# Two chained blocks on one core: steps reordered at two branch ends, in the wide feed-forward network and in attention

## The chip, the cores and the metric

The kernel runs on 1 core of one Trainium2 chip. The metric is the device time of one execution in microseconds (us); the time before is the median of three runs, 3123.27 us (3117.45 to 3126.45). All numbers are f32. The engines, each with an instruction stream of its own, are TensorE (PE: matmuls and, with an identity matrix, transposes; PEld in a profile is its weight load), VectorE (DVE), ScalarE (ACT), GpSimd (POOL) and SyncE (SP), which issues most of the DMAs.

## The reference

Two blocks are chained, each with two layers, on 256 tokens of 1024 features. What matters here:

```python
def first_block(x, ...):            # 2 layers
    x = layer_norm(a * x + 0.5 * swiglu(x, w1, w3, w2))        # FFN, 2816 hidden features
    x = layer_norm(a * x + token_mixing(x, ...))
    x = layer_norm(a * x + 0.5 * swiglu(x, ...))
    x = layer_norm(a * x + sigmoid(x @ ple_gate) * (p @ ple_proj))

def token_mixing(x, ...):
    h_rw, h_gla, h_gdn, h_gate = split(x @ w_in)
    o_rw  = rwkv7(h_rw)
    o_gla = gated_linear_attention(h_gla)   # per head: rms_norm(o) * silu(gate)
    o_gdn = gated_delta_net(h_gdn)          # per head: rms_norm(o) * silu(gate)
    proj  = [o_rw @ w_b[0], o_gla @ w_b[1], o_gdn @ w_b[2]]    # branches, 512 -> 1024
    return sum(sigmoid(h_gate)[n] * proj[n] for n in range(3)) @ w_o

def second_block(h, c, hc):         # hc: 256 context tokens
    # layer 0: attention, 16 query heads, 4 key and value heads of 64 features
    h  += g1  * (softmax(q_l @ [k_c, k_l].T / 8) @ [v_c, v_l]) @ w_o
    hc += g1c * (softmax(q_c @ k_c.T / 8) @ v_c) @ w_o
    h  += g2  * swiglu(mod(rms_norm(h)),  w_in, w_out)         # the same weights
    hc += g2c * swiglu(mod(rms_norm(hc)), w_in, w_out)         # for both streams
    # layer 1: HGRN2 in place of attention, and a swiglu; h alone
    return rms_norm(h)
```

## The kernel before, in words

Each engine's order is written out by hand: a function `pe_x`, `act_x`, `dve_x` issues what that engine does in stage x, and semaphores join them (`wait_ge` waits, `then_inc` and `sem_inc` count up). Nothing is scheduled by a compiler, so an instruction waits for all that stands ahead of it on its engine. TensorE's results go through eight banks of PSUM: `to_dve` hands out four that VectorE empties, `to_act` four that ScalarE empties; `filled` and `freed` count them. Weights come through a ring of three slots. SP issues their loads in order, each as soon as TensorE marks a slot as used (`used`, and `release` at the next matmul).

All matmuls are recorded at line 460 and all transposes at 463, so they are told apart by tile and shape. Each f32 matmul stands as two rows of TensorE in the trace.

*Feed-forward networks* (`pe_ffn7`, `act_ffn7`, `dve_ffn7`) multiply 2x2 blocks by a scheme of seven products. The sums of weight blocks (`dve_T`, L802), of hidden blocks (`hidden_sum`, L812) and of the products in their banks (`add`, L899: the bank sums) are VectorE's. The hidden K tiles come in groups of 4, 4 and 3, and for each group TensorE takes the products 1, 2, 6, 5, 3, 4, 7; product 6 waits for weight sums, and two products of the last group wait until VectorE has taken a bank. The wide network is that of the second block's layer 0: it runs over two streams (latents and context) and two halves of the output features. While half 1 of stream 0 ends (`more`), VectorE makes the hidden sums of stream 1 too.

*Branch ends.* `pe_branch` turns tile 0 of the normalized branch output, multiplies half of its product, turns tile 1 and goes on. ScalarE copies the turned tile (`act_branch_turned`, L1437), VectorE normalizes by head (`dve_head_std`, L1849 to 1865) with a square root from ScalarE (`act_head_std`, L1631) and multiplies by the gate (`dve_branch_gate`, L2400). ScalarE loads a function's table before its first use (ACT_TABLE_LOAD); `act_prepare_sqrt` (L1059) loads one ahead by a small Sqrt. In `pe_gla`, `STEPS` says how many K steps of the late sigmoid gates stand between the stages of the second branch. In `act_gdn`, L2542 is the Silu of the third branch's gate.

*Attention* goes by units: 16 of stream 0 (the latents, 128 queries by 512 keys, two heads) and 8 of stream 1 (the context, 256 queries by 256 keys, two heads). For each, TensorE makes the scores; VectorE takes row maxima (L3635) and scales them (L3638); ScalarE takes Exps with row sums (L3542); VectorE normalizes (L3645, L3649); TensorE turns the probabilities; ScalarE and VectorE copy these (L3554, L3657); TensorE weighs the values with them (`weigh`), three units behind the scores; and the weighed values are copied (`keep_o`, L3663 on VectorE), four units behind. Ahead of the units stand projections, norms and turned tiles of queries and keys, by tile (`qk_tile_ready`).

Of the kernel before, what the change touches and what calls it, by code (L numbers as in the profile page):

```python
# [19 lines left out]
ACT = mybir.ActivationFunctionType  # L20
# [3 lines left out]
P = 128  # L24
# [102 lines left out]
def two_blocks(nc, a, out):  # L127
    ctx = ExitStack()
    with ctx:
# [104 lines left out]
        values_weighed = sem("values_weighed")  # L234
        qkT_ready = sem("qkT_ready")
        qk_norm_landed = sem("qk_norm_landed")
# [586 lines left out]
        def dve_ffn7(dve, apply, early_rows=None, in_down=None, join_last=False):  # L823
# [53 lines left out]
            for half in range(2 * w.streams):  # L877
# [179 lines left out]
        def act_prepare_sqrt(act):  # L1057

            ins = act.e.activation(small[:, 60:61], ones[:, 0:1], ACT.Sqrt)  # L1059
            ins.then_inc(act_step, act.up(act_step))  # L1060
            act.wait_ge(act_step, act.sent(act_step))
# [1195 lines left out]
        def act_gla(act):  # L2257
# [150 lines left out]
        def pe_gla(pe):  # L2408
# [11 lines left out]
            late = {}  # L2420
            STEPS = (3, 2, 2, 2, 2, 1, 0, 1, 0, 3)

# [86 lines left out]
        def act_gdn(act):  # L2509
# [76 lines left out]
        def dve_gdn(dve):  # L2586
# [110 lines left out]
            for tt in range(2):  # L2697
                for c in range(2):
# [53 lines left out]
                    dve.wait_ge(to_dve.freed, dve.sent(to_dve.freed))  # L2752
                    if (tt, c) == (1, 1):
                        dve.wait_ge(gdn_gate_ready, dve.due(gdn_gate_ready))
                        dve_norm_gate(dve, 1, gdn_gate[:, 1], dG[:].rearrange("p t h n -> p (t h n)"))
                        continue
# [618 lines left out]
        def pe_attention(pe):  # L3375
# [3 lines left out]
            for n in range(5):  # L3379
# [13 lines left out]
                pe.wait_ge(qk_tile_ready, pe.due(qk_tile_ready))  # L3393
                for src, nq in ((qk_tok[:, QKV_ORDER[n - 1]], 2), (kk[:].rearrange("p a b -> p (a b)"), 1)):
                    for q in range(nq):
                        pe.wait_ge(to_act.freed, to_act.next_free())
                        bank = to_act.free_bank()
                        for k in range(4):
# [4 lines left out]
                            if k == 3:  # L3403
                                mm.then_inc(to_act.filled, 1)
# [4 lines left out]
            pe.wait_ge(qkT_ready, pe.due(qkT_ready))  # L3409
            units = attention_units()  # L3410
# [25 lines left out]
            def weigh(u):  # L3436
# [15 lines left out]
            for u in range(len(units) + 3):  # L3452
# [4 lines left out]
                if u >= 3:  # L3457
                    weigh(u - 3)
            pe.wait_ge(oT_ready, pe.due(oT_ready))
            for half in range(2):  # L3460
                blk = pe.block()
# [29 lines left out]
        def act_attention(act):  # L3491
            e = act.e
            for n in range(5):
# [15 lines left out]
                else:  # L3509
                    t0 = QKV_ORDER[n - 1] * P  # L3510
                    for dst, nq in ((qT, 2), (kT, 1)):
                        for q in range(nq):
# [11 lines left out]
                if n == 3:  # L3524
                    for tt in range(4):
                        act.wait_ge(to_act.filled, to_act.next_filled())
                        bank = to_act.filled_bank()
                        e.copy(av_tok[:, tt], bank[:, 0:256]).then_inc(to_act.freed, act.up(to_act.freed))
                        act.wait_ge(to_act.freed, act.sent(to_act.freed))
            act.sem_inc(qkT_ready, act.up(qkT_ready))  # L3530
            units = attention_units()

            def exps(u):
# [3 lines left out]
                act.wait_ge(scores_ready, u + 1)  # L3537
                act.wait_ge(max_ready, act.due(max_ready))
                bias, total = by_query(u, am[:, 0:8]), by_query(u, am[:, 8:16])
                for j in range(2 if s == 0 else 4):  # L3540
                    src = score_pair(u)[:, j] if s == 0 else score_pair(u)[:, j // 2, j % 2 * SEQ:(j % 2 + 1) * SEQ]
                    ins = e.activation(probs(u, j), src, ACT.Exp, scale=0.125, bias=bias[:, j:j + 1],  # L3542
                                       accum_out=total[:, j:j + 1])
# [14 lines left out]

            for u in range(len(units) + 2):
                if u >= 2:  # L3560
                    keep_PT(u - 2)
                if u < len(units):
                    exps(u)

        def dve_attention(dve):
# [3 lines left out]
            for tt in QKV_ORDER:  # L3569
# [55 lines left out]
                if tt == QKV_ORDER[0]:  # L3625
                    dve_keep_gate_rows(dve, (0, 1))
            dve.wait_ge(qk_tile_turned, dve.due(qk_tile_turned))
            units = attention_units()

            def maxes(u):  # L3630
                dve.wait_ge(scores_ready, u + 1)
                src = score_pair(u)
                if units[u][1]:
                    src = src.rearrange("p r (q n) -> p r q n", q=2)
                ins = v.tensor_reduce(by_query(u, am[:, 16:24]), src, AX.X, ALU.max)  # L3635
                ins.then_inc(dve_step, dve.up(dve_step))
                dve.wait_ge(dve_step, dve.sent(dve_step))
                ins = v.tensor_scalar(by_query(u, am[:, 0:8]), by_query(u, am[:, 16:24]), -0.125, None, ALU.mult)  # L3638
                ins.then_inc(max_ready, dve.up(max_ready))
                dve.wait_ge(max_ready, dve.sent(max_ready))  # L3640

# [19 lines left out]
            def keep_o(n):  # L3661
                dve.wait_ge(values_weighed, n + 1)
                ins = v.tensor_copy(oT[:, n % 8, n // 8 * SEQ:(n // 8 + 1) * SEQ], psum[n % 2][:, 0:SEQ])  # L3663
# [1028 lines left out]
```

## Time and profile before

| what | value |
|---|---|
| median of three runs | 3123.27 us (3117.45 to 3126.45) |
| the profiled execution | 3114.14 us, span 3112.4 us |
| mean granted clock of TensorE in it | 0.989 of full speed |
| instructions | 53034 |
| busy: TensorE, VectorE, ScalarE, GpSimd | 2980.6, 1758.1, 708.4, 43.6 us |
| share of the weight queue in the DMA engines' time | 39.1%; 429.92 MB in all |

The profile is of one execution, in microseconds from the span's start; the time of that execution includes what lies around the span. A busy TensorE is not necessarily at full clock: the granted clock is given apart, and 0.50 is the lower of its two levels, 1.2 GHz, beside 2.4.

### The profile page before, as it was taken

The page shows a single profiled execution, that of the slowest core. Times are in us where ns is not written, and L with a number is a line of the kernel's source. Part 1 is how long each engine was busy: PE and PEld are TensorE (multiplying, and loading weights), DVE is VectorE, ACT ScalarE, POOL GpSimd, SP SyncE. Part 2 cuts the span into 40 slices and gives each one's busy share as a digit, 9 for nine tenths or more (in the row PEclk, how much of TensorE's full clock was granted, in tenths as well). Part 3 has the DMA queues.
Part 4 walks back from the last instruction along what each step waited for, and adds up shares of the span by engine and source line. Part 5 has one row for each costly group of instructions (what it writes and reads, how often), then busy time and mean ns, then how long its engine had stood idle before and what let it go on. Part 6 is the DMA issues. An engine that isn't in the chain of part 4 may idle for free. (4 is left out here: it accounts for less than half of the span.)

```text
span 3112.4 us, 53034 instructions
## 1 busy us (share of the span) xinstructions
PE 2980.6 (96%) x22878; PEld 2362.2 (76%) x22878; DVE 1758.1 (56%) x2604; ACT 708.4 (23%) x1354; POOL 43.6 (1%) x83
## 2 busy tenths in 40 slices
PE   8999998999999999999999999989999999998998
PEld 8987774559977998684558984555888887765897
DVE  5554556446646564465446556584333664486665
ACT  2102114211112101213212104272111012254210
POOL 1000000000001000000000000000000000000000
PEclk9999999999999999999999999999999999998999
DMA  8745312237556755323227643201222343331543
GB/s 285 234 162 184 135 58 97 80 122 243 188 183 203 249 176 187 135 70 109 82 82 236 230 154 134 81 1 54 82 81 93 138 154 110 108 109 62 163 163 109
DMA packets 279818, 429.92 MB, mean 138 GB/s; under 512 B 10073, under 2 KB 147777, under 8 KB 279585
## 3 DMA queue, kind: packets, MB, share of 16 engines
q1 hardware_dynamic: 273936, 411.52, 39.1%
q0 software_dynamic: 5024, 13.82, 1.4%
q8 instruction: 182, 2.98, 0.4%
q10 hardware_dynamic: 624, 1.19, 0.1%
q14 instruction: 52, 0.42, 0.0%
HBM read 425.45 MB, written 1.05 MB: 137 GB/s over the span
## 5 line engine op out<-in xcount | busy, mean ns | idle before, releaser
L460 PE MATMUL bank<-arena 64*64 64x64 f32 (+9 forms) x7292 | 744.0, 284 | 36.6 <-DVE arena L2359 5.8
L460 PEld LDWEIGHTS bank<-arena 128*128 128x128 f32 (+4 forms) x7292 | 641.8, 163 | 135.9 <-issue 32.1
L460 PE MATMUL bank<-xT,ring 128*128 128x128 f32 (+2 forms) x4512 | 723.2, 319 | 10.0 <-DVE arena L842 5.7
L460 PEld LDWEIGHTS bank<-xT,ring 128*128 128x128 f32 (+1 forms) x4512 | 655.7, 191 | 70.8 <-issue 10.1
L460 PE MATMUL bank<-ring,xT 128*128 128x512 f32 (+3 forms) x1632 | 581.7, 527 | 4.2 <-DVEq L1098 2.0
L460 PEld LDWEIGHTS bank<-ring,xT 128*128 128x128 f32 (+1 forms) x1632 | 266.0, 183 | 261.3 <-issue 242.1
L460 PE MATMUL bank<-ring,arena 128*128 128x256 f32 (+1 forms) x1584 | 442.6, 431 | 22.1 <-issue 11.2
L460 PEld LDWEIGHTS bank<-ring,arena 128*128 128x128 f32 x1584 | 300.3, 191 | 137.2 <-issue 89.9
L842 DVE TENSOR_TENSOR arena<-arena,bank 128x256 f32<-128x256 f32 (+1 forms) x198 | 92.2, 466 | 394.8 <-PE bank L460 255.6
L753 ACT COPY arena<-bank 128x256 f32<-128x256 f32 (+1 forms) x264 | 107.6, 408 | 746.8 <-PE bank L460 745.5
L802 DVE TENSOR_TENSOR arena<-ring,arena 128x1024 f32<-128x1024 f32 (+1 forms) x216 | 257.1, 1190 | 7.4
L802 DVE TENSOR_TENSOR arena<-ring 128x1024 f32<-128x1024 f32 (+1 forms) x108 | 129.6, 1200 | 92.9 <-PE bank L460 88.2
L460 PE MATMUL bank<-arena,ring 128*128 128x128 f32 (+1 forms) x1152 | 168.2, 300 | 0.0
L460 PEld LDWEIGHTS bank<-arena,ring 128*128 128x128 f32 x1152 | 154.4, 192 | 7.0
L460 PE MATMUL bank<-xT,arena 128*128 128x128 f32 (+1 forms) x1104 | 158.0, 296 | 0.2 <-DVE arena L842 0.2
L460 PEld LDWEIGHTS bank<-xT,arena 128*128 128x128 f32 x1104 | 145.2, 192 | 6.2 <-DVE arena L842 0.4
L802 DVE TENSOR_TENSOR ring<-ring 128x1024 f32<-128x1024 f32 (+1 forms) x108 | 128.6, 1191 | 3.7
L463 PEld LDWEIGHTS bank<-cst,arena 128*128 128x128 f32 x482 | 54.8, 142 | 40.0 <-DVE arena L3649 24.0
L463 PE MATMUL bank<-cst,arena 128*128 128x128 f32 x482 | 68.1, 279 | 12.0 <-DVEq L3659 7.9
L783 ACT COPY arena<-bank 128x256 f32<-128x256 f32 x14 | 5.2, 372 | 325.1 <-PE bank L460 325.1
L899 DVE TENSOR_TENSOR arena<-arena,bank 128x256 f32<-128x256 f32 x56 | 23.6, 421 | 78.9 <-PE bank L460 77.6
L831 DVE TENSOR_TENSOR arena<-arena 128x512 f32<-128x512 f32 (+1 forms) x66 | 51.6, 781 | 25.3 <-ACT arena L772 20.7
(411 smaller groups left out, 2131.2 us busy)
## 6 DMA issues: line engine op xcount, KB each, us to landing
ring<-in_ffn_w SPq DMA_DIRECT2D x88, 1024.0 KB, 8.0
ring<-in_w_in SPq DMA_DIRECT2D x32, 2048.0 KB, 7.8
ring<-in_ffn_w_in SPq DMA_DIRECT2D x44, 1024.0 KB, 6.8
arena<-in_ada_w SPq DMA_DIRECT2D x20, 2048.0 KB, 13.8
ring<-in_ffn_w SPq DMA_DIRECT2D x16, 2048.0 KB, 8.0
ring<-in_ffn_w_out SPq DMA_DIRECT2D x12, 2048.0 KB, 7.9
ring<-in_hgrn_w_in SPq DMA_DIRECT2D x12, 2048.0 KB, 7.9
ring<-in_ffn_w SPq DMA_DIRECT2D x8, 1536.0 KB, 6.7
```

The lines of the kernel that those rows point to most:

```text
L460: return self.e.matmul(o, lhsT, rhs, start=start, stop=stop, skip_group_check=True)
L463: return self.e.transpose(o, x, ident[0:n, 0:n])
L753: ins = e.copy(w.s[:, i], bank[:, 0:w.T])
L783: e.copy(w.kept[:, 0], banks[0][:, 0:256]).then_inc(down_kept, act.up(down_kept))
L802: v.tensor_tensor(out_, a_, b_, ALU.subtract).then_inc(T_sums, dve.up(T_sums))
L831: ins = v.tensor_tensor(w.hid_block(b), c4[:, :, :, 0], c4[:, :, :, 1], ALU.mult)
L842: ins = v.tensor_tensor(out_, kept, c, ALU.add)
L899: v.tensor_tensor(out_, a_, b_, ALU.add).then_inc(done, dve.up(done))
```

## The change

Five edits; all results that are computed stay the same.

1. Wide feed-forward network, half 1 of stream 0: the hidden sums of the second group of stream 1 go from ahead of the bank sums to behind them, and those of the third group from ahead of a set of weight sums to behind it.
2. End of the second branch: ScalarE copies the turned tile 0 ahead of the Sqrt table's load.
3. In the same stage one K step of the late gates goes from ahead of output tile 0 to behind it.
4. End of the third branch: ScalarE loads the Silu table behind the first square root; VectorE takes the second tile's squares ahead of its wait for the gate.
5. Attention: the last value tile's projection is split in two and its second half goes behind the last turned tiles; the last turned keys are copied by VectorE; the Exp table is loaded ahead by a small Exp; the first unit's maxima are taken in two halves, each followed by its Exp; the outputs of stream 1 are copied by ScalarE, behind the Exps of its round, and `weigh` waits for that copy.

The core of the diff:

```diff
@@ dve_ffn7
-                if more:
-                    for i in range(4):
-                        hidden_sum(s + 1, 1, i)
                 if half and in_down:
                     in_down()
...
                 dve.sem_inc(down_read, dve.up(down_read))
                 if more:
                     for i in range(4):
-                        hidden_sum(s + 1, 2, i)
+                        hidden_sum(s + 1, 1, i)
                 if half < last:
                     dve_T(dve, f, t0 + 4)
+                if more:
+                    for i in range(4):
+                        hidden_sum(s + 1, 2, i)
@@ act_gla
+            act_branch_turned(act, 0, cols[:, GLAG:GLAG + 1])
             act_prepare_sqrt(act)
-            act_branch_turned(act, 0, cols[:, GLAG:GLAG + 1])
             act_head_std(act)
@@ pe_gla
-            STEPS = (3, 2, 2, 2, 2, 1, 0, 1, 0, 3)
+            STEPS = (3, 2, 2, 2, 2, 1, 0, 0, 1, 3)
@@ act_gdn
                 act_head_std(act)
+                if tt == 0:
+                    act_prepare_silu(act)
@@ dve_gdn
                     if (tt, c) == (1, 1):
+                        squares = ...
+                        dve_head_std(dve, head_view(1), squares, 4)
                         dve.wait_ge(gdn_gate_ready, dve.due(gdn_gate_ready))
-                        dve_norm_gate(dve, 1, gdn_gate[:, 1], ...)
+                        dve_branch_gate(dve, 1, gdn_gate[:, 1])
@@ pe_attention
                 if n == 3:
                     for tt in range(4):
-                        pe_tok(pe, blks[2], to_act, 256, 256, x_lhs, (tt,))
+                        pe_tok(pe, blks[2], to_act, 256, 128 if tt == 3 else 256, x_lhs, (tt,))
+                if n == 4:
+                    pe_tok(pe, blks[2], to_act, 384, 128, x_lhs, (3,))
                     pe.used()
...
-                if n >= 2 and qt == 0:
+                if n >= 10:
+                    pe.wait_ge(kept_by_act, pe.due(kept_by_act))
+                elif n >= 2 and qt == 0:
                     pe.wait_ge(values_kept, n - 1)
@@ act_attention
+            e.activation(small[:, 60:61], ones[:, 0:1], ACT.Exp).then_inc(act_step, act.up(act_step))
...
+            def keep_o(i):
+                act.wait_ge(values_weighed, 8 + i + 1)
+                ins = e.copy(oT[:, i, SEQ:2 * SEQ], psum[i % 2][:, 0:SEQ])
+                ins.then_inc(kept_by_act, act.up(kept_by_act))
...
                 if u < len(units):
                     exps(u)
+                if u >= 4 and units[u - 4][1]:
+                    keep_o(units[u - 4][0])
@@ dve_attention
-                if s or qt:
-                    keep_o(8 * s + i)
+                if s == 0 and qt:
+                    keep_o(i)
```

Where the instructions stand, first on VectorE in the wide network, half 1 of stream 0. L802 is a weight sum, L812 a hidden sum, L899 (896 in the changed kernel) a bank sum. Before:

```order
L812 TENSOR_TENSOR arena<-arena 128x4x128 x4
L802 TENSOR_TENSOR arena<-ring 128x1024
L802 TENSOR_TENSOR arena<-ring,arena 128x1024 x2
L802 TENSOR_TENSOR ring<-ring 128x4x256
L812 TENSOR_TENSOR arena<-arena 128x4x128 x4
L899 TENSOR_TENSOR arena<-arena,bank 128x256 x2
L899 TENSOR_TENSOR arena<-arena 128x256
L899 TENSOR_TENSOR arena<-arena,bank 128x256
```

And the changed kernel in the same place, and then, some residual steps later, the sums that follow:

```order
L812 TENSOR_TENSOR arena<-arena 128x4x128 x4
L802 TENSOR_TENSOR arena<-ring 128x1024
L802 TENSOR_TENSOR arena<-ring,arena 128x1024 x2
L802 TENSOR_TENSOR ring<-ring 128x4x256
L896 TENSOR_TENSOR arena<-arena,bank 128x256 x2
L896 TENSOR_TENSOR arena<-arena 128x256
...
L812 TENSOR_TENSOR arena<-arena 128x4x128 x4
L802 TENSOR_TENSOR arena<-ring 128x1024
L802 TENSOR_TENSOR arena<-ring,arena 128x1024 x2
L802 TENSOR_TENSOR ring<-ring 128x4x256
L812 TENSOR_TENSOR arena<-arena 128x3x128 x4
```

The second group's sums (4 K tiles, 128x4x128) stand behind the bank sums now, ahead of the weight sums; those of the third group (128x3x128), which stood there, come behind these.

The second place is ScalarE at the end of the second branch. L1437 (1443) copies a turned tile, L1059 is the load of the Sqrt table with its small Sqrt, L1631 (1637) the square root of a head's mean square. Before:

```order
L1380 ACTIVATE xT<-bank 128x2x256
L1059 ACT_TABLE_LOAD
L1059 ACTIVATE small<-cst 128x1
L1437 ACTIVATE arena<-bank,cols 128x4x128
L1631 ACTIVATE small<-small 128x4
```

The changed kernel:

```order
L1386 ACTIVATE xT<-bank 128x2x256
L1443 ACTIVATE arena<-bank,cols 128x4x128
L1059 ACT_TABLE_LOAD
L1059 ACTIVATE small<-cst 128x1
L1637 ACTIVATE small<-small 128x4
```

The copy has passed the load and the small Sqrt; the square root stands where it stood.

The third place is ScalarE at the end of the third branch. L2542 (2548) is the Silu of a gate, L1065 of the changed kernel the small Silu. Before:

```order
L1631 ACT_TABLE_LOAD
L1631 ACTIVATE small<-small 128x4
L2542 ACT_TABLE_LOAD
L2542 ACTIVATE arena<-bank 128x512
L1437 ACTIVATE arena<-bank,cols 128x4x64 x2
```

The changed kernel:

```order
L1637 ACT_TABLE_LOAD
L1637 ACTIVATE small<-small 128x4
L1065 ACT_TABLE_LOAD
L1065 ACTIVATE small<-cst 128x1
L2548 ACTIVATE arena<-bank 128x512
L1443 ACTIVATE arena<-bank,cols 128x4x64 x2
```

The number of table loads is the same; the second stands with the small Silu, which waits for nothing, where it stood with the Silu, which waits for a bank.

## Rows read from the trace of the kernel before

**Rows 1.** The page, busy time of each engine with its share and instructions.

```profile
PE 2980.6 (96%) x22878; PEld 2362.2 (76%) x22878; DVE 1758.1 (56%) x2604; ACT 708.4 (23%) x1354; POOL 43.6 (1%) x83
```

**Rows 2.** Waits of TensorE: us in total, times, longest.

```profile
PE bank L460 <- issue: 18.3, 14, 2.7
```

**Rows 3.** Timeline, wide network: start, us, instructions, [idle before, releaser].

```profile
2461.62 1.56 PE L460 MATMUL bank<-ring,arena 128*128 128x256 f32 x6 [0.44 <-DVE arena L899]
2464.31 1.89 PE L460 MATMUL bank<-ring,arena 128*128 128x256 f32 x8
...
2495.02 2.87 DVE L812 TENSOR_TENSOR arena<-arena 128x512 f32<-128x512 f32 x4
2498.58 2.03 PE L460 MATMUL bank<-ring,arena 128*128 128x256 f32 x6 [3.46 <-DVE arena L899]
2502.96 4.91 PE L460 MATMUL bank<-ring,arena 128*128 128x256 f32 x22
2517.49 1.23 DVE L802 TENSOR_TENSOR ring<-ring 128x1024 f32<-128x1024 f32 x1
2519.80 1.46 PE L460 MATMUL bank<-arena 128*128 128x256 f32 x6
```

**Rows 4.** Timeline, end of the second branch, layer 0 and layer 1.

```profile
538.93 1.28 ACT L1059 ACT_TABLE_LOAD   x1
540.46 0.69 ACT L1437 ACTIVATE arena<-bank,cols 128x512 f32<-128x512 f32 x1
541.29 3.67 PE L460 MATMUL bank<-ring,arena 128*128 128x512 f32 x8 [2.66 <-issue]
542.60 0.69 DVE L2400 TENSOR_TENSOR arena<-arena 128x512 f32<-128x512 f32 x1
544.80 0.60 PE L463 MATMUL bank<-cst,arena 128*128 128x128 f32 x4
...
1492.95 5.19 PE L460 MATMUL bank<-ring,arena 128*128 128x512 f32 x8 [2.66 <-issue]
```

**Rows 5.** Timeline, end of the third branch, layer 0 and layer 1.

```profile
647.67 1.28 ACT L2542 ACT_TABLE_LOAD   x1 [9.57 <-PE bank L460]
648.09 0.66 PE L463 MATMUL bank<-cst,arena 128*128 128x128 f32 x4
649.68 0.98 ACT L1437 ACTIVATE arena<-bank,cols 128x256 f32<-128x256 f32 x2
650.81 3.67 PE L460 MATMUL bank<-ring,arena 128*128 128x512 f32 x8 [2.06 <-issue]
...
1604.86 5.37 PE L460 MATMUL bank<-ring,arena 128*128 128x512 f32 x8 [2.06 <-issue]
```

**Rows 6.** Timeline, the first attention unit.

```profile
2010.47 1.99 PE L460 MATMUL bank<-arena 64*128 64x512 f32 x8 [1.21 <-ACTq L3530]
2011.72 1.22 DVE L3635 TENSOR_REDUCE arena<-bank 128x2 f32<-128x1024 f32 x1 [5.62 <-PE bank L460]
2014.52 0.69 ACT L3542 ACTIVATE arena<-bank,arena 128x512 f32<-128x512 f32 x1
2016.16 2.08 PE L460 MATMUL bank<-arena 64*128 64x512 f32 x4 [3.70 <-ACT arena L3542]
```

**Rows 7.** Timeline, attention's second stream: VectorE over one unit.

```profile
2086.90 1.23 DVE L3635 TENSOR_REDUCE arena<-bank 128x4 f32<-128x1024 f32 x1
2090.64 0.42 DVE L3663 COPY arena<-bank 128x256 f32<-128x256 f32 x1
2091.10 1.23 DVE L3635 TENSOR_REDUCE arena<-bank 128x4 f32<-128x1024 f32 x1
```

**Rows 8.** Groups by line and shape: a bank's copy on ScalarE (busy, mean ns).

```profile
L753 ACT COPY arena<-bank 128x256 f32<-128x256 f32 x220 | 81.9, 372 | 539.6 <-PE bank L460 538.5 <-ACT xT L3157 0.2
```

**Rows 9.** Windows: us, busy of PE, PEld, DVE, ACT, POOL, clock, DMA share, GB/s.

```profile
1492.70:1495.90 3.20, 2.94 (x4) 1.43 (x5) 1.56 (x3) 0.41 (x2) 0.00 (x0) 0.50 0.00 0
2014.90:2021.60 6.70, 5.44 (x16) 2.58 (x16) 3.49 (x8) 4.54 (x12) 0.00 (x0) 0.50 0.09 27
```

More of the change, by code:

```diff
@@ L1059, in act_prepare_sqrt, with act_prepare_silu @@
             ins = act.e.activation(small[:, 60:61], ones[:, 0:1], ACT.Sqrt)
+            ins.then_inc(act_step, act.up(act_step))
+            act.wait_ge(act_step, act.sent(act_step))
+        def act_prepare_silu(act):
+            ins = act.e.activation(small[:, 60:61], ones[:, 0:1], ACT.Silu)
             ins.then_inc(act_step, act.up(act_step))
@@ L2753, in dve_gdn @@
                     if (tt, c) == (1, 1):
+                        squares = dG[:].rearrange("p t h n -> p (t h n)").rearrange("p (h n) -> p h n", h=4)
+                        dve_head_std(dve, head_view(1), squares, 4)
                         dve.wait_ge(gdn_gate_ready, dve.due(gdn_gate_ready))
-                        dve_norm_gate(dve, 1, gdn_gate[:, 1], dG[:].rearrange("p t h n -> p (t h n)"))
+                        dve_branch_gate(dve, 1, gdn_gate[:, 1])
                         continue
@@ L3394, in pe_attention @@
                 for src, nq in ((qk_tok[:, QKV_ORDER[n - 1]], 2), (kk[:].rearrange("p a b -> p (a b)"), 1)):
+                    banks = to_dve if n == 4 and nq == 1 else to_act
                     for q in range(nq):
-                        pe.wait_ge(to_act.freed, to_act.next_free())
-                        bank = to_act.free_bank()
+                        pe.wait_ge(banks.freed, banks.next_free())
+                        bank = banks.free_bank()
                         for k in range(4):
@@ L3459, in pe_attention @@
             pe.wait_ge(oT_ready, pe.due(oT_ready))
+            pe.wait_ge(kept_by_act, pe.due(kept_by_act, 2))
             for half in range(2):
@@ L3510, in act_attention @@
                     t0 = QKV_ORDER[n - 1] * P
-                    for dst, nq in ((qT, 2), (kT, 1)):
+                    for dst, nq in ((qT, 2), (kT, 1)) if n < 4 else ((qT, 2),):
                         for q in range(nq):
@@ L3527, in act_attention @@
                         bank = to_act.filled_bank()
-                        e.copy(av_tok[:, tt], bank[:, 0:256]).then_inc(to_act.freed, act.up(to_act.freed))
+                        w = 128 if tt == 3 else 256
+                        e.copy(av_tok[:, tt, 0:w], bank[:, 0:w]).then_inc(to_act.freed, act.up(to_act.freed))
                         act.wait_ge(to_act.freed, act.sent(to_act.freed))
-            act.sem_inc(qkT_ready, act.up(qkT_ready))
+            act.sem_inc(kept_by_act, act.up(kept_by_act))
+            act.wait_ge(to_act.filled, to_act.next_filled())
+            bank = to_act.filled_bank()
+            e.copy(av_tok[:, 3, 128:256], bank[:, 0:128]).then_inc(to_act.freed, act.up(to_act.freed))
+            act.wait_ge(to_act.freed, act.sent(to_act.freed))
+            e.activation(small[:, 60:61], ones[:, 0:1], ACT.Exp).then_inc(act_step, act.up(act_step))
+            act.wait_ge(act_step, act.sent(act_step))
             units = attention_units()
@@ L3557, in keep_PT @@
                     act.sem_inc(PT_ready, act.up(PT_ready))
-            for u in range(len(units) + 2):
-                if u >= 2:
+            def keep_o(i):
+                act.wait_ge(values_weighed, 8 + i + 1)
+                ins = e.copy(oT[:, i, SEQ:2 * SEQ], psum[i % 2][:, 0:SEQ])
+                ins.then_inc(kept_by_act, act.up(kept_by_act))
+                act.wait_ge(kept_by_act, act.sent(kept_by_act))
+            for u in range(len(units) + 4):
+                if 2 <= u < len(units) + 2:
                     keep_PT(u - 2)
@@ L3626, in dve_attention @@
                     dve_keep_gate_rows(dve, (0, 1))
+            t0 = QKV_ORDER[3] * P
+            dve.wait_ge(to_dve.filled, to_dve.next_filled())
+            bank = to_dve.filled_bank()
+            ins = v.tensor_copy(kT[:, :, t0:t0 + P], bank[:].rearrange("p (k t) -> p k t", k=4))
+            ins.then_inc(to_dve.freed, dve.up(to_dve.freed))
+            dve.wait_ge(to_dve.freed, dve.sent(to_dve.freed))
             dve.wait_ge(qk_tile_turned, dve.due(qk_tile_turned))
@@ L3634, in maxes @@
                     src = src.rearrange("p r (q n) -> p r q n", q=2)
[L3635 to L3640, printed above, removed]
+                top, bias = by_query(u, am[:, 16:24]), by_query(u, am[:, 0:8])
+                for q in ((0, 1), (1, 2)) if u == 0 else ((0, top.shape[1]),):
+                    q_ = slice(*q)
+                    ins = v.tensor_reduce(top[:, q_], src[:, q_] if u == 0 else src, AX.X, ALU.max)
+                    ins.then_inc(dve_step, dve.up(dve_step))
+                    dve.wait_ge(dve_step, dve.sent(dve_step))
+                    ins = v.tensor_scalar(bias[:, q_], top[:, q_], -0.125, None, ALU.mult)
+                    ins.then_inc(max_ready, dve.up(max_ready))
+                    dve.wait_ge(max_ready, dve.sent(max_ready))
             def scale(u):
```

13 lines of the change are left out of this document (8 added, 5 removed).

## The prediction

> **What bounds the kernel now.** I began with the page's busy line: TensorE works for 96% of the span and VectorE for little over half [rows 1], so the time falls only where TensorE waits, or where it runs at its lower clock. I therefore read the waits of TensorE next. Its largest heading is a wait that the profile can't put down to a finished instruction ("issue"): 14 gaps of together 18.3 us, the longest 2.7 [rows 2]. Then I went through the timeline at the five places that the diff touches. Four gaps of that heading lie there: 2.66 us ahead of the second branch's product, in both layers [rows 4], and 2.06 us ahead of the third's, in both layers [rows 5]. The two others are 3.46 us in the wide FFN, where TensorE waits for a bank sum of VectorE [rows 3], and 3.70 us at the first attention unit, where it waits for ScalarE's Exps [rows 6]. Last I asked for the granted clock behind these gaps. Four of the six are followed by a stretch at 0.50 of the clock, which is 1.2 instead of 2.4 GHz; two of the four stand in [rows 9], and the stretches from 1605.3 and from 2499.6 show the same 0.50. A product of eight instructions takes 5.19 or 5.37 there, and 3.67 at full clock [rows 4, 5]. So a gap removed can be worth more than its length.
>
> **Part A, the wide FFN's hidden sums.** Before, four hidden sums (2.87 us) stand on VectorE ahead of the bank sums that TensorE waits for. The block before, where nothing stands there, has a gap of 0.44 in the same place; this one has 3.46 [rows 3]. Removed: 3.46 − 0.43 = 3.03. The clock: from the end of the gap to the next product's start is 2502.96 − 2498.58 = 4.38 here and 2464.31 − 2461.62 = 2.69 there; if the short gap doesn't lower the clock, another 1.69 goes. Against it: the four sums now stand ahead of the next weight sums (four operations, of which the last is the 1.23 at 2517.49). These ended at 2518.72, and TensorE took product 6 at 2519.80, with 1.08 to spare [rows 3]. After the change TensorE is there 4.7 earlier, at about 2515.1. VectorE comes to its bank sums 2.87 earlier and, with TensorE at full clock, waits some 0.5 less behind them. But the four sums ahead of these weight sums are now those over 512 columns instead of those over 384, which is at most a quarter of 2.87, 0.7, and I take 0.5. So the weight sums end 2.9 earlier, at about 2515.8. That is a new gap of about 0.75; the bounds are 0 and 2.9, the whole of the moved sums. Part A: 3.03 + 1.69 − 0.75 = 4.0.
>
> **Part B, the end of the second branch.** ScalarE loads the Sqrt table at 538.93, warms it up, and only at 540.46 copies the turned tile for which TensorE's product waits, to 541.29 [rows 4]. With the copy first it starts 1.53 earlier, and so does the product, at 539.76. Behind the product's first half TensorE turns the second tile. That needs VectorE's gate product, which ends at 542.60 + 0.69 = 543.29 and which doesn't come sooner, since ScalarE still has the same work ahead of the square root it rests on. So the turn goes from 544.80 to about 543.36 and the gain is 1.44, with hardly any waiting left over. Layer 1 has the same 1.44, and its slow product (5.19 − 3.67) gives another 1.52 if the shorter gap leaves the clock up. Part B: 2 × 1.44 + 1.52 = 4.4; the bounds are 0 (the turn is late by as much) and 2 × 1.53 + 1.52 = 4.6.
>
> The Trainium skill ("ScalarE: Activation LUTs", section "What ACT_TABLE_LOAD costs") adds a drain of about 1.38 us to each load of 1.28. In the trace load, warm-up and both waits fit into the 1.53 between 538.93 and 540.46 [rows 4], so no such drain is paid here. By the page, parts B and D would gain 1.38 more in each layer, 5.5 in all.
>
> **Part C, the moved gate step.** One step is two of the instructions of which eight take 3.67 [rows 4], so 0.92. It goes from ahead of the first output tile to behind it. TensorE does as much before it turns the first tile, and ScalarE's copy still waits for the last steps, so I take 0; the bounds are ±0.9 for each layer.
>
> **Part D, the end of the third branch.** ScalarE had waited 9.57 us, loads the Silu table at 647.67 for 1.28, computes the last gate, and copies the turned tile at 649.68; the product starts at 650.81 [rows 5]. With the table loaded in the idle time, the gate is done 1.28 earlier. But the turned tile lands only at 648.09 + 0.66 = 648.75, so the copy starts at about 648.82 and the product at 649.95: 0.86. The gate product that the second turn needs comes about as much earlier, because VectorE's squares no longer wait for the gate. Layer 1 likewise, and there 5.37 − 3.67 = 1.70 more at full clock. Part D: 2 × 0.86 + 1.70 = 3.4; the bounds are 0 and 2 × 1.28 + 1.70 = 4.3.
>
> **Part E, attention.** The start: the value matmuls that move fill TensorE's wait for the last turned keys, and VectorE takes over one copy; I take +0.2 (bounds −0.6, an unhidden copy, and +1.2, the wait of 1.21 ahead of the first scores [rows 6]). From the first scores to the third scores it takes 2016.16 − 2010.47 = 5.69. The maximum of both halves (1.22, begun 1.25 behind the first scores), a table load and two Exps lie between [rows 6]. After it: 1.25 to the first half's maximum, about 0.69 + 0.2 for it, two Exps of 0.69 with their sums, and the table is there already: about 3.9, so 1.8 less. That the clock is at 0.50 from 2014.9 to 2021.6 [rows 9] gives up to 0.8 more if it stays up. The first stream then runs at ScalarE's pace and carries the gain on. In the second stream a unit takes 2091.10 − 2086.90 = 4.20 and VectorE, which sets it, has no idle time; the output's copy takes 2091.10 − 2090.64 = 0.46 of it [rows 7]. ScalarE makes such a copy in 0.372 [rows 8] and has some 0.5 to spare in a unit. Four units still have maxima behind the copy: 4 × 0.46 = 1.8, and the tail loses about 0.2. Part E: 0.2 + 1.8 + 0.4 (half of the clock's 0.8) + 1.8 + 0.2 = 4.4, bounds 1.0 and 7. A weight load that SP now issues behind attention is hidden by the output products that TensorE starts with the same wait; without that cover it would cost its landing, some microseconds.
>
> For plain elementwise work the Trainium skill ("ScalarE: Activation LUTs", section "Rules for kernel authors") advises VectorE, up to about three times as fast in bf16. The f32 rows here disagree: 0.372 on ScalarE [rows 8], 0.42 on VectorE [rows 7]. By the rule the copy would take up to 1.27 on ScalarE, 0.8 more than a unit has room for, and the second stream would lose 4 × 0.8 = 3.2 where I count 1.8 won.
>
> **Sum.** 4.0 + 4.4 + 0 + 3.4 + 4.4 = 16.2. Of this 1.69 + 1.52 + 1.70 + 0.8 = 5.7 would hang on the clock, of which part E counts only half; for slow stretches that come back or appear elsewhere I take 1.2 off. So 15.0, and the profiled execution would go from 3114.14 to 3099. That execution is 9.1 under the median of the three runs, 3123.27, and the forecast goes by the median: 3108.
>
> **Rivals.** *The clock is redrawn.* Two equal gaps of 2.66 were followed by full clock in layer 0 and by half in layer 1 [rows 4], and likewise those of 2.06 [rows 5], so the length of a gap alone doesn't decide it. If the same share of slow stretches returns in other places, 5.7 of the 16.2 stay out: 10.5, so 3112.8. Against it: the stretches follow gaps, and all six gaps shrink. 18%.
>
> *Waits move instead of going.* TensorE waits the full 2.9 for the weight sums in part A (2.2 more than counted), and ScalarE with its added copy sets the second stream (−2.0). 12 left, so 3111.2. For it: VectorE has only 1.08 of slack there [rows 3] and ScalarE some 0.5. 14%.
>
> *Slower: the loop of attention closes.* TensorE's weighing in the second stream now waits for ScalarE's copy, and that copy stands in ScalarE's order behind four Exps of the current unit. If the weighing of unit u−3 waits for the copy of the same round, then all of a unit runs one after another. What that costs the first unit shows, which has no overlap: 5.69 from scores to scores [rows 6]. Its table load of 1.28 falls away; two more Exps, the copy and a weighing come in, by estimate 2.5 together: 6.9 instead of 4.20. With TensorE at 0.50 behind such gaps, as in [rows 9], its part of the loop, scores (2.08 at 0.50 [rows 6], so 1.04 at full clock) and about as long a weighing, is some 2.1 longer: 9.0. Six units at 4.8 more make 29 us; the other parts and the start of attention still win 4.0 + 4.4 + 3.4 + 2.4 − 1.2 = 13, so 3123.27 + 29 − 13 = 3139. By my count the weighing waits for the copy of one round earlier, which is done when it is wanted; one place off in that count decides. 6%.
>
> **Numbers.** Forecast 62%, the rivals 18, 14 and 6. The spread of the three runs is about ±4.5, and 0.3%, 9.4 us, is what can be told from no change. Below 3113.9 the kernel is faster: nearly nine in ten of the forecast, about six in ten of the first two rivals' share: 0.74. The same: 0.21. Slower: 0.05. The range goes from 3099 (the upper bounds of parts D and E, with a low draw) to 3117 (the second rival with a high draw); what lies above is the third rival and little else.
>
> **What would show it.** A: a gap of about 0.4 where 3.46 stood, full clock behind it, and a gap under 1 at the next product 6. B and D: products 1.4 and 0.9 us earlier against the turn ahead of them, with 3.67 for eight instructions in both layers. E: a first unit of about 3.9, a second-stream unit of about 3.75, and no gap at weighing. The forecast is wrong if the mean clock falls below that of before, if the unit of the second stream is over 4.2, or if TensorE's product 6 waits for over 2 us.

## The result, and the profile after

The changed kernel takes 3100.70 us by the median of four runs (3097.66 to 3101.51), against 3121.68 for before: 0.9931 of its time, with a 95% interval of 0.9913 to 0.9948. That is 21 us less; the forecast was 15 less, 3108, with a range of 3099 to 3117. The profiled execution took 3101.1 us, span 3099.3, at a mean granted clock of 0.991, where before's had 3114.14 and 0.989. Of the 58 runs of before beside the experiments below one took 5185.31 us, at a mean granted clock of 0.555; it is left out of every figure here.

All five places look as forecast. The wide network, in the timeline of the changed kernel (start, us, instructions, idle time before with its releaser), answers to [rows 3]:

```profile
2488.28 1.56 PE L460 MATMUL bank<-ring,arena 128*128 128x256 f32 x6 [0.37 <-DVE arena L896]
2490.98 4.91 PE L460 MATMUL bank<-ring,arena 128*128 128x256 f32 x22
...
2500.47 2.87 DVE L812 TENSOR_TENSOR arena<-arena 128x512 f32<-128x512 f32 x4
2507.26 1.22 DVE L802 TENSOR_TENSOR ring<-ring 128x1024 f32<-128x1024 f32 x1
2508.54 3.72 PE L460 MATMUL bank<-arena 128*128 128x256 f32 x16 [0.57 <-DVE ring L802]
```

The gap of 3.46 is 0.37; from its end to the next product it takes 2490.98 − 2488.28 = 2.70, as at full clock. The moved sums now stand ahead of the weight sums, and product 6 waits for these: 0.57, where 0.75 was put down.

The ends of the branches (timeline of the changed kernel, second branch in layer 0 and layer 1, then the third in both) answer to [rows 4, 5]:

```profile
542.55 0.69 ACT L1443 ACTIVATE arena<-bank,cols 128x512 f32<-128x512 f32 x1
543.34 1.28 ACT L1059 ACT_TABLE_LOAD   x1
543.39 3.67 PE L460 MATMUL bank<-ring,arena 128*128 128x512 f32 x8 [1.21 <-issue]
544.64 0.20 ACT L1059 ACTIVATE small<-cst 128x1 f32<-128x1 f32 x1
546.21 0.69 DVE L2406 TENSOR_TENSOR arena<-arena 128x512 f32<-128x512 f32 x1
546.96 0.66 PE L463 MATMUL bank<-cst,arena 128*128 128x128 f32 x4
...
1495.38 3.67 PE L460 MATMUL bank<-ring,arena 128*128 128x512 f32 x8 [1.21 <-issue]
...
651.55 0.66 PE L463 MATMUL bank<-cst,arena 128*128 128x128 f32 x4
652.25 0.98 ACT L1443 ACTIVATE arena<-bank,cols 128x256 f32<-128x256 f32 x2 [0.50 <-PE bank L463]
653.37 3.67 PE L460 MATMUL bank<-ring,arena 128*128 128x512 f32 x8 [1.16 <-issue]
...
1603.92 3.67 PE L460 MATMUL bank<-ring,arena 128*128 128x512 f32 x8 [1.16 <-issue]
```

The gaps are 1.21 for 2.66 and 1.16 for 2.06, all four products take 3.67, and ScalarE waits for the turned tile (0.50) and no longer for a table. The second turn of the second branch starts right behind the gate product, 546.21 + 0.69 = 546.90: that product has become its limit, as forecast.

Attention, in the timeline of the changed kernel, answers to [rows 6, 7]:

```profile
2007.29 1.99 PE L460 MATMUL bank<-arena 64*128 64x512 f32 x8 [0.40 <-issue]
2008.55 0.69 DVE L3678 TENSOR_REDUCE arena<-bank 128x1 f32<-128x512 f32 x1 [2.72 <-PE bank L460]
2009.56 0.69 ACT L3568 ACTIVATE arena<-bank,arena 128x512 f32<-128x512 f32 x1 [0.85 <-DVE arena L3681]
2011.28 1.50 PE L460 MATMUL bank<-arena 64*128 64x512 f32 x4 [2.00 <-ACT arena L3568]
...
2069.39 1.23 DVE L3678 TENSOR_REDUCE arena<-bank 128x4 f32<-128x1024 f32 x1
2073.60 1.23 DVE L3678 TENSOR_REDUCE arena<-bank 128x4 f32<-128x1024 f32 x1
2077.34 1.23 DVE L3678 TENSOR_REDUCE arena<-bank 128x4 f32<-128x1024 f32 x1
2077.61 0.37 ACT L3587 COPY arena<-bank 128x256 f32<-128x256 f32 x1
2081.09 1.23 DVE L3678 TENSOR_REDUCE arena<-bank 128x4 f32<-128x1024 f32 x1
2084.83 1.23 DVE L3678 TENSOR_REDUCE arena<-bank 128x4 f32<-128x1024 f32 x1
```

From the first to the third scores it takes 3.99 (5.69 before; 3.9 forecast), and a unit of the second stream 2077.34 − 2073.60 = 3.74 (4.20 before; 3.75 forecast). Three units are that short; the one from 2069.39 still takes 4.21. Behind five of the six shortened gaps this profile has the full clock. Behind that of attention it has not (window; us, busy of PE, PEld, DVE, ACT, POOL, then the granted clock, DMA share, GB/s):

```profile
2012.00:2015.30 3.30, 3.09 (x12) 1.99 (x12) 3.07 (x8) 2.36 (x6) 0.00 (x0) 0.50 0.00 0
```

If one lays the turned tiles of the two profiles side by side, the steps add up to 3.9 for the wide network, 1.4 and 3.0 for the second branch, 0.9 and 2.6 for the third, and 4.6 for attention: 16.4, against 16.2 in the forecast. Yet the two profiled executions lie only 13 apart, since the clock fell in the changed kernel's at places where it had not before, and the medians lie 21 apart. What stands between 13, 16 and 21 is the question of the experiments.

### The profile page after: what moved, and what is told of

Read it like the earlier page. It is cut to its first block and busy times, and to the rows that moved or that the text cites. A ratio compares the mean times of both kernels' runs of the same rounds, so it can differ in the third digit from the quotient of the medians.

```text
span 3099.3 us, 53073 instructions
## 1 busy us (share of the span) xinstructions
PE 2976.3 (96%) x22894; PEld 2359.3 (76%) x22894; DVE 1755.8 (57%) x2599; ACT 711.5 (23%) x1365; POOL 43.7 (1%) x83
## 3 DMA queue, kind: packets, MB, share of 16 engines
q8 instruction: 182, 2.98, 0.4%
## 5 line engine op out<-in xcount | busy, mean ns | idle before, releaser
L460 PEld LDWEIGHTS bank<-xT,ring 128*128 128x128 f32 (+1 forms) x4512 | 655.7, 191 | 71.2 <-issue 10.5
L802 DVE TENSOR_TENSOR arena<-ring,arena 128x1024 f32<-128x1024 f32 (+1 forms) x216 | 257.2, 1191 | 7.4
L802 DVE TENSOR_TENSOR arena<-ring 128x1024 f32<-128x1024 f32 (+1 forms) x108 | 129.6, 1200 | 89.6 <-PE bank L460 84.7
L802 DVE TENSOR_TENSOR ring<-ring 128x1024 f32<-128x1024 f32 (+1 forms) x108 | 128.6, 1191 | 3.7
```

The lines of the kernel that those rows point to most:

```text
L460: return self.e.matmul(o, lhsT, rhs, start=start, stop=stop, skip_group_check=True)
L802: v.tensor_tensor(out_, a_, b_, ALU.subtract).then_inc(T_sums, dve.up(T_sums))
```

## The experiments

A number that they need: each run has its mean granted clock c, and 2 × (1 − c) × span is the time that TensorE stood at the lower of its two levels, called us at the lower clock below. The clock is recorded to three places, so this is good to about 3 us in one run, and means over runs are compared. Over 57 runs of before, taken beside these experiments, it is 82 us on average, and a line through those runs gives 0.42 us of run time for each us at the lower level.

**The parts alone.** Four kernels, each the kernel before with one edit (in short). The moved gate step (edit 3) had no kernel of its own.

```diff
 e1: -  hidden_sum(s + 1, 1, i) ahead of the bank sums
     +  hidden_sum(s + 1, 1, i) behind them; hidden_sum(s + 1, 2, i) behind dve_T(t0 + 4)
 e2: -  act_prepare_sqrt(act); act_branch_turned(act, 0, ...)
     +  act_branch_turned(act, 0, ...); act_prepare_sqrt(act)
 e3: +  if tt == 0: act_prepare_silu(act)      # and dve_head_std ahead of the gate's wait
 e4: all of the edit in attention
```

> Edit 1 alone (hidden sums of the wide network behind the bank sums). My theory: the gap ahead of the third product falls from 3.46 to about 0.4 us, the stretch behind it is at full clock, and product 6 waits 0.6 to 0.8 us for the weight sums: 4.0 us less between the two streams of that network than in the trace of before, nothing elsewhere but other draws of the clock; so 3118 by the median of before (3121.7). Rival (the measured 21 us are no draws but real gains that my sum of 16 missed, and lie in this part): 6 us or more less in this stretch. Rival (waits move): product 6 waits over 2 us, and 2 us are left.

> Edit 2 alone (the copy of the turned tile ahead of the Sqrt table at the end of the second branch), without the moved gate step. My theory: 1.4 us less between the first turn and the products behind the second, in each layer, and 1.5 more in layer 1 if its product is at full clock: 2.9 to 4.4. If the moved gate step had a part in that (rival), this kernel wins less than 1.2 per layer, or more. Median by the theory about 3118.

> Edit 4 alone (Silu table loaded early, squares of the second tile ahead of the gate). My theory: the product starts 0.86 us earlier against the turn ahead of it, in both layers, with 1.7 more in layer 1 at full clock: 1.7 to 3.4. By a drain of 1.38 us behind each table load, which would be saved too, 2.2 per layer at full clock. Median by the theory about 3119.

> Edit 5 alone (attention). My theory: 4.4 us less from the last projections of attention to the first output product, 1.5 to 2 of it before the first unit's end, 1.8 to 2.6 in the second stream, whose unit takes 3.75 instead of 4.20. Rival (ScalarE becomes the bound there): a unit of 4.2 and 2 us less in all. Median by the theory about 3117.

| kernel | median (10 runs) | ratio, 95% interval | us at the lower clock |
|---|---|---|---|
| hidden sums alone | 3117.91 | 0.9991 (0.9982 to 1.0001) | 79 |
| second branch's copy alone | 3113.76 | 0.9977 (0.9968 to 0.9987) | 72 |
| third branch's table alone | 3117.87 | 0.9989 (0.9979 to 0.9998) | 73 |
| attention alone | 3117.97 | 0.9988 (0.9979 to 0.9997) | 80 |

Before had 3121.70 beside them, at 80 us at the lower clock. The first part's interval includes no change, and those of the last two end close to it. The second part takes 7.9 us off, where 2.9 to 4.4 were expected; it stands 8 us less at the lower clock than before did, so by the line above about 3 us of that are the clock's. In the traces the steps stand as they did together: 3.9 in the wide network (product 6 waits 0.57), 1.44 and 2.98 in the second branch (1.44 and 2.97 in the whole change), 0.90 and 2.60 in the third, and 3.5 in attention, where the slow stretch behind the first unit stayed as long as in the first profile of before. From its first turned tile to its second the second branch wins without the moved gate step what it won with it, so the step shows no effect there. The four ratios together take 0.55% or 17 us off, and the whole 0.69%: the same within the intervals. So the rival that one part hides a large gain falls.

The Trainium skill ("ScalarE: Activation LUTs", section "What ACT_TABLE_LOAD costs") has a drain of 1.38 us beside each load of 1.28. By it, the expectation for the third branch put 2.2 us per layer beside 0.86, and the trace has 0.90. That gain ends at the wait for the turned tile, so it can't decide. The rows of the second branch above do: the load ends at 543.34 + 1.28 = 544.62, and the next activation starts at 544.64. No such drain stands in this trace, and the measurement decides.

**The changed kernel again.** Not an edit; for the clock of more runs.

> The changed kernel as it is, once more. Over the 30 runs of before so far, TensorE stood at the lower clock for 80 us of a run on average (from its mean clock, 0.987), and from run to run a us of that costs 0.38 us. My theory now: of the 21 us measured, only 9 to 10 are waits removed (2.4 to 3.5 for each of the parts but the gate step) and the rest is the clock, of which I had counted a third: this kernel stands at the lower clock for 50 to 58 us, and 3100 +- 2 comes again. Rival: the four runs so far were lucky draws; then clock and time go towards 0.989 and 3106.

It took 3101.22 (four runs, ratio 0.9937, 0.9913 to 0.9961), as expected. These four stand at the lower clock for 60 us, a little above the 50 to 58 expected, where the first four had 53; one of them has the rival's figures (3105.35, 0.989), the other three have not. All eight runs have 57 us on average, against 82. By the line through the runs of before, the 25 us less are worth an estimated 25 × 0.42 = 10.5, so of 21 us half would be the clock and half the waits removed. The next experiment tests that.

**Idle time filled, waits kept.** The kernel before, with dummy work for TensorE in just the gaps that the change shortens (the code in short).

```diff
+        def pe_fill(pe, banks, n):
+            pe.wait_ge(banks.freed, banks.next_free())
+            bank = banks.banks[banks.opened % len(banks.banks)]
+            for k in range(n):
+                pe.turn(bank[:, k % 4 * P:(k % 4 + 1) * P], ident[:])
...
             # pe_branch, ahead of the first product (second and third branch)
+            pe_fill(pe, to_dve, 15 if between else 20)
             # and 26 turns into psum[4] ahead of product 3 of the wide network's half 1,
             # 28 into psum[0] ahead of the third scores of attention
```

> The kernel before, none of its waits removed, with dummy transposes of the identity (results unread, into a free bank) in the six gaps that the change shortens: 20 in each of the two of 2.66 us, 15 in each of 2.06, 26 in that of 3.46 and 28 in that of 3.70. My theory (of the 21 us, 9 to 10 are waits removed, and the rest is the clock, which falls where TensorE idles): with the idling gone and the waits kept, the time at the lower clock falls from 80 to some 60 us, and about 8 us are won, 3113. Rival (the clock has nothing to do with these gaps): 78 to 84 us at the lower clock and 3120 to 3124.

It took 3112.68 (five runs; 0.9964, 0.9951 to 0.9977): 8.6 us faster than the 3121.31 of before beside it, though no wait of the kernel was removed and TensorE does more. It had 56 us at the lower clock. The changed kernel has as much, 57, and takes 3101.2: the 11.5 us between these two are the removed waits without the clock. In the traces these are the 16.4 of the steps less the 4.9 of the three places that are back at full clock (1.69, 1.52 and 1.70, as the prediction has them): 11.5. Beside it ran the kernel before for a second profile:

> The kernel before once more, for a second profile: the first was among the fastest of its runs. Theory: 75 to 85 us at the lower clock and 3118 to 3124, with stretches at 0.50 behind most of the six gaps that the change shortens. Rival: 69 us as in the first profile, and then the clock explains nothing of the distance between that profile and the median.

It took 3123.16. The two side by side, first that second profile of before (windows; us, busy of PE, PEld, DVE, ACT, POOL, then the granted clock, DMA share, GB/s), behind the six gaps in order of time:

```profile
546.20:549.40 3.20, 3.20 (x4) 1.40 (x5) 1.56 (x3) 0.18 (x1) 0.00 (x0) 0.50 0.08 8
658.80:662.10 3.30, 3.30 (x6) 1.24 (x5) 1.56 (x3) 0.92 (x2) 0.00 (x0) 0.50 0.33 88
1501.90:1505.20 3.30, 2.71 (x4) 1.19 (x5) 1.56 (x3) 0.74 (x2) 0.00 (x0) 0.50 0.00 0
1617.95:1621.20 3.25, 3.25 (x5) 1.35 (x4) 1.56 (x3) 0.66 (x2) 0.00 (x0) 0.50 0.53 133
2027.60:2030.80 3.20, 3.20 (x12) 2.07 (x12) 2.72 (x6) 2.01 (x6) 0.00 (x0) 0.50 0.00 0
2508.85:2512.10 3.25, 2.81 (x7) 2.27 (x8) 1.23 (x3) 0.00 (x0) 0.00 (x0) 0.50 0.00 0
```

The same places with the gaps filled, in the same columns:

```profile
546.80:550.20 3.40, 3.40 (x8) 1.55 (x9) 1.56 (x3) 0.29 (x1) 0.00 (x0) 1.00 0.34 73
656.30:659.70 3.40, 3.40 (x8) 1.46 (x9) 1.90 (x4) 1.56 (x2) 0.00 (x0) 1.00 0.27 75
1499.10:1502.50 3.40, 3.40 (x8) 1.58 (x9) 1.56 (x3) 0.30 (x1) 0.00 (x0) 1.00 0.28 53
1608.40:1612.00 3.60, 3.40 (x8) 1.45 (x9) 2.13 (x4) 1.69 (x3) 0.00 (x0) 1.00 0.25 47
2018.30:2021.50 3.20, 3.10 (x16) 1.41 (x16) 2.92 (x7) 2.73 (x6) 0.00 (x0) 1.00 0.00 0
2500.20:2503.40 3.20, 3.20 (x15) 2.84 (x16) 2.29 (x5) 0.00 (x0) 0.00 (x0) 1.00 0.02 5
```

Six of six at 0.50, and six of six at full clock. The timeline of the second profile of before shows what that is worth at the first of them:

```profile
542.80 0.66 PE L463 MATMUL bank<-cst,arena 128*128 128x128 f32 x4
546.12 5.37 PE L460 MATMUL bank<-ring,arena 128*128 128x512 f32 x8 [2.66 <-issue]
551.32 0.60 PE L463 MATMUL bank<-cst,arena 128*128 128x128 f32 x4
```

And with the gap filled:

```profile
543.51 0.66 PE L463 MATMUL bank<-cst,arena 128*128 128x128 f32 x4
544.00 2.35 PE L463 MATMUL bank<-cst 128*128 128x128 f32 x20
546.78 3.70 PE L460 MATMUL bank<-ring,arena 128*128 128x512 f32 x8 [0.43 <-ACTq L1454]
550.31 0.60 PE L463 MATMUL bank<-cst,arena 128*128 128x128 f32 x4
```

The product waits as long for its tile (546.78 − 543.51 = 3.27 from the turn ahead of it, 546.12 − 542.80 = 3.32 without the dummies), and then takes 3.70 instead of 5.37. Over the whole trace the two kernels drift 10.5 us apart. The six places make 10.2 of it, 0.9 to 3.1 each; at other places the kernels drift by up to 2.3 us one way or the other, which cancels. That TensorE idled is what lowered the clock there; the rival, that the clock has nothing to do with these gaps, falls.

**Filling other waits.** The changed kernel with dummies in other waits of TensorE (in short).

```diff
 e6: +            pe_fill(pe, to_dve, 40)          # ahead of turn_readout(0)
 e7: e6 and 7 ahead of each branch's first product, 5 and 14 ahead of the second branch's
     last two levels, 14 at the end of transitions without a condition product
 e10: e7, and dve_T(t0 + 4) ahead of both groups of hidden sums
 e12: e7, and 14 ahead of the third scores of attention
```

> The changed kernel with 40 dummy transposes of the identity on TensorE, into a free bank, in the wait of 5.2 us ahead of the turns of the HGRN readout (2842 us), whose results nobody reads. If the clock falls because TensorE stood idle: no stretch at 0.50 behind that wait (10.2 us in the changed kernel's profile), the output product behind it takes 7 and not 9.9 us, and 4 us are saved, 3096. Rival (the fall has to do with load or power over longer times, or the dummies delay the turns): the stretch stays, and 0 to 2 us are lost.

> As the one before, with dummies also in the waits behind the first turn of each branch (7), ahead of the last two levels of the second branch's decay (5 and 14) and at the end of transitions without a condition product (14). If idling lowers the clock: time at the lower clock falls from some 53 to 30 us, and by 0.38 us each 9 us are saved, 3091; where a dummy still runs when the work is there, some tenths are lost. Rival: the clock is drawn for other reasons, its time stays at 50, and the dummies cost 1 to 3 us.

> The changed kernel with the dummies of the seventh run, and in the wide network the weight sums ahead of both groups of moved hidden sums. Theory: the wait of 0.57 us at product 6 goes, time at the lower clock stays near 40 us, 3097 by the median, 3 to 4 under the changed kernel. Rival (the seventh run was a lucky draw, and dummies do nothing): 52 to 58 us at the lower clock, 3100.

> The seventh run's kernel (the changed kernel with dummy transposes in four kinds of waits; the wide network's order as in the changed kernel) with 14 more dummies in the wait of 2.0 us ahead of the third scores of attention. Theory: 36 to 42 us at the lower clock, 3097 +- 2, 3 to 4 under the changed kernel. Rival (the seventh run was a lucky draw): 50 us or more at the lower clock, 3100 or more.

| kernel | median (runs) | ratio, 95% interval | us at the lower clock |
|---|---|---|---|
| one wait filled (e6) | 3099.98 (4) | 0.9928 (0.9908 to 0.9948) | 51 |
| many (e7) | 3097.99 (4) | 0.9921 (0.9901 to 0.9940) | 40 |
| many, weight sums first (e10) | 3102.94 (6) | 0.9930 (0.9917 to 0.9944) | 49 |
| one more wait (e12) | 3097.78 (5) | 0.9924 (0.9910 to 0.9938) | 51 |

None came out as expected. The single fill won 1.2 us on the 3101.22 beside it, not 4. Many fills won 3 where 9 were expected, with 40 us at the lower clock for 30. The third kernel was to take 3097 and took 3102.94. The last took the time expected, but has 51 us at the lower clock, where 36 to 42 were forecast and its rival put 50 or more. By the line through the runs of before, 17 us less than the changed kernel at the lower clock (e7) should win 7 us and 6 us less (e12) 2.5; both win about 3.

Behind the single fill the product still ran slow (timeline of that kernel, then the granted clock of two windows).

```profile
2833.60 4.59 PE L463 MATMUL bank<-cst 128*128 128x128 f32 x40
2838.91 0.65 PE L463 MATMUL bank<-cst,ctok 128*128 128x128 f32 x4 [0.72 <-DVE ctok L4395]
2840.57 0.66 PE L463 MATMUL bank<-cst,ctok 128*128 128x128 f32 x4 [1.01 <-DVE ctok L4395]
2842.00 10.05 PE L460 MATMUL bank<-ring,xT 128*128 128x512 f32 x16 [0.78 <-ACTq L4224]
...
2841.40:2844.70 3.30, 2.70 (x3) 1.17 (x4) 3.13 (x6) 1.10 (x3) 0.00 (x0) 0.50 0.00 0
2848.20:2851.50 3.30, 3.30 (x9) 1.39 (x9) 0.00 (x0) 0.00 (x0) 0.00 (x0) 1.00 1.11 356
```

The wait of 5.24 was filled up to 0.72, but three gaps of 0.7 to 1.0 still lie between short turns, and the 16 instructions took 10.05 where 9.87 stood. The turns are faster (0.65 for 1.11), and the stretch at 0.50 is shorter, 6.8 us for 10.2, but nearly all of it falls on the product. One filled wait is no promise where others follow; why the clock fell there is open. Filling many gives two kernels at 3098 (e7 and e12), three us under the changed kernel. One was timed side by side with the changed kernel (3097.99 to 3101.22), the other apart; the intervals overlap, so they are probably faster, not surely.

Kernel e10 shows that the order chosen in the change matters. With the weight sums first, the wait at product 6 goes, as expected, but the hidden sums come too late for the first product of the next group (its timeline):

```profile
2504.79 1.23 DVE L809 TENSOR_TENSOR ring<-ring 128x1024 f32<-128x1024 f32 x1
2506.05 5.35 DVE L819 TENSOR_TENSOR arena<-arena 128x512 f32<-128x512 f32 x8
2509.13 6.70 PE L460 MATMUL bank<-ring,arena 128*128 128x256 f32 x16 [4.06 <-DVEq L845]
```

A wait of 0.57 became one of 4.06, with a slow stretch behind it, and that network lost 6.5 us against the changed kernel.

**The closed loop.** The changed kernel with the outputs' copies one round later, as the third rival would have it.

```diff
-                if u >= 4 and units[u - 4][1]:
-                    keep_o(units[u - 4][0])
+                if u >= 5 and units[u - 5][1]:
+                    keep_o(units[u - 5][0])
```

> The changed kernel with ScalarE's copies of the second stream's outputs one round later, so that TensorE's weighing waits for the copy of its own round, behind four Exps: the closed loop of my third rival. By its price a unit takes 6.9 to 9.0 us instead of the 3.75 measured, for six units 19 to 31 us more. Rival: VectorE and TensorE still work ahead in the other units, a unit takes under 5, and 3 to 8 us are lost.

It took 3122.73 in its one run. In its timeline TensorE's weighing waits for the copy and is slow (3.99 for 16 instructions that take 2.15 in the changed kernel's units):

```profile
2087.32 3.99 PE L460 MATMUL bank<-arena 128*64 128x256 f32 x16 [3.41 <-ACT arena L3587]
...
2095.98 3.98 PE L460 MATMUL bank<-arena 128*64 128x256 f32 x16 [3.43 <-ACT arena L3587]
```

A unit takes 2095.98 − 2087.32 = 8.66, within the 6.9 to 9.0 of the rival's price. It is near the upper price, which has TensorE at the lower clock, and the granted clock is 0.50 from 2095.5 to 2102. But the loop closes for three units and not for six: the first copies still come early, and behind the last scores nothing is left to hold up. So it cost 14 us in that stage and not 19 to 31; the rest of the 21.5 us to the changed kernel's 3101.22 lies at other places, in this one run. The mechanism and the unit's price were right, the count wrong, and one place in an index is all that keeps the kernel out of it.

## Why the prediction was right, and where it was small

*The waits.* Part A: the gap is 0.37 for 0.43 forecast, the new wait 0.57 for 0.75, the sum 3.9 for 4.0. Part B: 1.4 and 3.0, sum 4.4 as forecast; part C: nothing, as put down; part D: 0.9 and 2.6, sum 3.5 for 3.4. Part E: 4.6 for 4.4, the first scores 0.55 earlier for 0.2, the first unit 1.7 shorter for 1.8, the second stream's unit 3.74 for 3.75. That part E's sum fits is partly luck: only three units are shorter, which makes 1.4 and not 1.8; the tail wins 0.9 and not 0.2; and of the clock's 0.4 nothing is left in the sum, for through the first stream ScalarE's Exps keep the lead of 2.25 that the start and the first unit gave (0.55 and 1.7). In the second stream ScalarE did not become the bound, TensorE did not wait the full 2.9, and the weighing did not wait for the copies: the second and the third rival did not come.

*The clock* is the term that was mis-sized. The forecast took 5.3 us of gain that hang on it (5.7, with half of attention's 0.8) and 1.2 off for slow stretches that come back: 4.1. It came from one profile of before, in which the clock fell behind four of the six gaps. That profile was of one of the fastest executions: 3114.14, where the median is 3121.7. The second profile of before has the fall behind six of six, and the kernel with filled gaps wins 0.9 to 3.1 us on it at each of them. The runs put the clock's share at an estimated 10.5 us (25 us less at the lower level), and the kernel with filled gaps has 8.6, measured alone. With 10.5 in place of 4.1 the forecast would have been 3102. The range held, with 3100.70 near its lower end.

The Trainium skill ("TensorE: Matmul & The Clock Gate", section "Terms") puts the penalty of throttled time at about that time times one minus the ratio of the clocks, which is half of it at the half rate. The 0.42 us for each us that the runs of before give is near that. TensorE waits in some of these stretches (busy 2.71 of 3.30 us in the third window of before above), which would make it less; no run separates that.

*The rivals.* The first, that the clock is redrawn, is half true: in the profile of the changed kernel stretches at 0.50 stand at 479, 530 and 1431 us that the first profile of before has not. But over eight runs they did not come back in like number (57 us for 82), and with the six gaps filled they were as few (56). This rival's price was also a little off: of the 5.7 that hang on the clock the sum counts only 5.3, so 10.9 would be left, 3112.4. And the second's 12 leaves out the 1.2 that the forecast takes off for the clock.

*Open.* Why some gaps of equal length are followed by the lower clock in one execution and not in the next was not settled, nor why the clock still fell behind the single fill in the last stage, nor why e7, at the lower clock for 11 us less than e12, is no faster. That filling beats the changed kernel rests on nine runs against eight that were not all made side by side.

## What to carry to other kernels

Where TensorE is 96% busy, a wait that is removed may be worth about twice its length (here 21 us for 11.5 of waits), because the product behind it ran at the lower clock: ask for the granted clock behind every gap, in more than one profile, and compare the profiled execution with the median before a price is taken from it. And when a copy is moved to an engine with time to spare, count by which round it is waited for: one round more made a gain of 0.46 us in a unit a loss of 4.9.

## What the runs showed of the hardware

Unread work can make a kernel faster. 124 dummy transposes in six gaps took 8.6 us off the kernel before, though each gap lasted as long as before: the products behind ran at 2.4 instead of 1.2 GHz. In the changed kernel, where the gaps are short already, the same in other places gave about 3 us at most.
